# Value products and gates with features on partitions, and probabilities normalised ahead of their transposes, in a hybrid attention block

## What is computed

```python
h = rms_norm(x, norm_gain[l])
proj = jnp.einsum('btd,de->bte', h, w_in[l])
qa, ka, va, ga, qb, kb, vb, gb, qi, ki, wi = jnp.split(proj, offsets, axis=-1)
out_a = chunked_relpos_attention(heads(qa, H_A), heads(ka, H_A), heads(va, H_A), rel_bias[l])
out_b = dsa_sparse_attention(heads(qb, H_B), heads(kb, H_B), heads(vb, H_B), qi, ki, wi, slopes)
ya = out_a.reshape(B, T, D_A) * jax.nn.silu(ga)
yb = out_b.reshape(B, T, D_B) * jax.nn.silu(gb)
x = x + jnp.einsum('bte,ed->btd', concatenate([ya, yb]), w_out[l])
return rms_norm(x, final_gain)
```

## Time and profile before

| What | us |
|---|---|
| median of 3 runs | 533.62 (533.39 to 534.5) |
| span of the profiled execution, first to last instruction | 532.2 |
| median of the runs less that span | 1.4 |
| TensorE busy | 523.9 |
| VectorE busy | 351.6 |
| ScalarE busy | 262.7 |

### The profile page before, as it was taken

The page is one execution under the profiler, slowest core; times in us unless marked ns, Lnnn a source line. Parts: engine busy times, 40 slices in busy tenths (PEclk is TensorE's granted clock), DMA queues, the critical chain, the costliest instruction groups (busy, mean ns, idle before and its releaser), DMA issues.

```text
span 532.2 us, 8174 instructions
## 1 busy us (share of the span) xinstructions
PE 523.9 (98%) x2795; PEld 452.4 (85%) x2795; DVE 351.6 (66%) x516; ACT 262.7 (49%) x381; POOL 28.5 (5%) x46
## 2 busy tenths in 40 slices
PE   9999999999999999999999999999999999999994
PEld 6899998888888888888888888888888888888883
DVE  6897785765667656668665767657576666756454
ACT  6875545344543344445364636354545444634342
POOL 1005042250000000000000000000000000000000
PEclk9999999999999999999999999999999999999999
DMA  8966976659556566654655554555444574766614
GB/s 291 380 197 191 284 223 193 196 174 276 172 189 193 197 198 189 188 187 149 197 159 161 178 173 158 163 173 179 158 158 159 179 265 151 237 196 189 200 47 158
DMA packets 60375, 102.45 MB, mean 193 GB/s; under 512 B 3504, under 2 KB 45376, under 8 KB 60096
## 3 DMA queue, kind: packets, MB, share of 16 engines
q1 hardware_dynamic: 58656, 96.68, 56.6%
q0 software_dynamic: 1264, 5.00, 3.3%
q10 hardware_dynamic: 432, 0.47, 0.3%
HBM read 99.24 MB, written 2.11 MB: 190 GB/s over the span
## 4 chain that ended last, share of the span: by engine, by line
PE 98%; DVE 0%; ACT 0%; DVEq 0%; issue 0%
PE acc L427 27%; PE acc L392 16%; PE acc L394 16%; PE acc L393 16%; PE acc L425 13%; PE aux L613 1%; PE aux L503 1%; PE acc L430 1%; PE acc L464 1%; PE aux L617 1%; PE aux L592 1%; PE aux L674 1%; PE aux L602 1%; PE acc L440 1%; PE acc L449 0%; PE aux L590 0%
## 5 line engine op out<-in xcount | busy, mean ns | idle before, releaser
L988 DVE TENSOR_TENSOR w_lo<-w_raw,w_hi 128x1024 fp32r<-128x1024 f32 x172 | 213.4, 1243 | 151.3 <-ACT w_hi L717 150.5
L717 ACT ACTIVATE w_hi<-w_raw 128x1024 fp32r<-128x1024 f32 x172 | 181.9, 1059 | 224.0 <-PE acc L394 111.0
L427 PE MATMUL acc<-acts,w_hi 128*128 128x512 f32 (+1 forms) x640 | 215.5, 387 | 0.0
L425 PE MATMUL acc<-acts,w_lo 128*128 128x256 f32 (+1 forms) x600 | 165.4, 276 | 0.0
L392 PE MATMUL acc<-w_hi,acts 128*128 128x512 f32 x376 | 148.1, 394 | 0.0
L394 PE MATMUL acc<-w_hi,acts 128*128 128x512 f32 x376 | 146.6, 390 | 0.0
L393 PE MATMUL acc<-w_lo,acts 128*128 128x512 f32 x376 | 146.3, 389 | 0.0
L427 PEld LDWEIGHTS acc<-acts,w_hi 128*128 128x128 f32 x640 | 119.0, 188 | 20.2
L425 PEld LDWEIGHTS acc<-acts,w_lo 128*128 128x128 f32 x600 | 113.3, 189 | 0.7
L394 PEld LDWEIGHTS acc<-w_hi,acts 128*128 128x128 f32 x376 | 70.6, 188 | 15.1
L393 PEld LDWEIGHTS acc<-w_lo,acts 128*128 128x128 f32 x376 | 70.7, 188 | 14.2
(11 more groups left out here) (173 smaller groups left out, 364.6 us busy)
## 6 DMA issues: line engine op xcount, KB each, us to landing
w_raw<-w_blocks SPq DMA_DIRECT2D x140, 512.0 KB, 3.7
w_raw<-wo_blocks SPq DMA_DIRECT2D x32, 512.0 KB, 4.0
w_raw<-w_blocks SPq DMA_DIRECT2D x8, 256.0 KB, 5.8
v<-x POOLq DMA_DIRECT2D x1, 2048.0 KB, 10.2
qk<-xT SPq DMA_DIRECT2D x7, 256.0 KB, 6.5
o<-ext_dram POOLq DMA_DIRECT2D x1, 1024.0 KB, 7.2
fgain<-final_gain POOLq DMA_DIRECT2D x1, 1024.0 KB, 7.9
out<-o SPq DMA_DIRECT2D x2, 512.0 KB, 3.0
```

What stands on the lines that cost most here:

```text
L425: nc.tensor.matmul(acc[:, bank:bank + n], w_lo4[:, u % RING, q, c], a_hi[:, k, tokens], start=False, stop=False)
L427: last = nc.tensor.matmul(whole, w_hi4[:, u % RING, q, c], acts[:, k, :, tokens], start=(k == 0), stop=(k == KT - 1))
L717: nc.scalar.activation(flat(w_hi[:, s, :, :]), w_raw[:, s, :], ACT.Copy).then_inc(hi_done, 1)
L988: nc.vector.tensor_tensor(flat(w_lo[:, s, :, :]), w_raw[:, s, :], flat(w_hi[:, s, :, :]).bitcast(f32), ALU.subtract).then_inc(lo_done, 1)
```

## The change

- The gate blocks 14 to 17 are made in feature layout (`feature_unit`) and multiplied by `rk`; SP loads their weights in that layout.
- Probabilities are multiplied by one over their sums (`normalise`) ahead of their transposes. TensorE waits for this, not for the exponentials.
- v is kept as `v0_hi`, `v0_lo` (tokens 0 to 127, split) and `v1`. The value products have v as the stationary operand and give features on partitions: for each pair two full-precision products with `pT1` and six of 256 columns with `pT_hi` and `pT_lo`. ScalarE makes `pT_hi` and VectorE `pT_lo` (`pT_rest`).
- ScalarE copies the value products out, times 0.5 (`output`); `gated` works on features; `y_hi` and `y_lo` read `o` in SBUF. `y_transposes` is gone.
- In blocks 10 to 13 ScalarE takes exponentials before `features_low`. x is fetched into the storage of `qk` after the last score. TensorE's loops over blocks 10 to 17 are written out.

The diff, cut to its core:

```diff
...
-            def transpose_pair(pair, used2):
-                pe.wait_ge(exp_done, pair + 1)
-                pe.wait_ge(aux_read[2], used2)
+            def transpose_pair(pair):
+                pe.wait_ge(normed, pair + 1)
+                pe.wait_ge(aux_read[2], pair + AUX23_PAIRS)
...
+            def value_pair(pair):
                 pe.wait_ge(aux_read[1], pair + (AUX1_PAIRS + 1))
-                pe.wait_ge(aux_read[3], used3)
+                pe.wait_ge(aux_read[2], pair + (AUX23_PAIRS + 1))
+                pe.wait_ge(aux_read[3], pair + AUX23_PAIRS)
+                heads = [slice(2 * pair * HD + h * HD, 2 * pair * HD + (h + 1) * HD) for h in range(2)]
+                for h, c in enumerate(heads):
+                    nc.tensor.matmul(aux[3][:, h * T + P:h * T + T], v1_flat[:, c], pT1[:, h, :],
+                                     start=(h == 0), stop=False, skip_group_check=True)
+                for h, c in enumerate(heads):
+                    dst = aux[3][:, h * T:h * T + T]
+                    rows_hi, rows_lo = pT_hi[:, h * T:h * T + T], pT_lo[:, h * T:h * T + T]
+                    nc.tensor.matmul(dst, v0_hi_flat[:, c], rows_hi, start=False, stop=False, skip_group_check=True)
+                    nc.tensor.matmul(dst, v0_lo_flat[:, c], rows_hi, start=False, stop=False, skip_group_check=True)
+                    last = nc.tensor.matmul(dst, v0_hi_flat[:, c], rows_lo, start=False, stop=(h == 1),
+                                            skip_group_check=True)
                 last.then_inc(pv_done, 1)
...
             for u in range(UNITS):
                 pe.wait_ge(ylo_done, u + 1)
                 unit(G_OUT, u)
-                if u + 3 < UNITS:
-                    y_transposes(u + 3)
...
+            def pT_out(pair):
                 act.wait_ge(pt_done, pair + 1)
+                nc.scalar.activation(pT_hi, aux[2][:, :], ACT.Copy).then_inc(pt_hi_done, 1)
+                nc.scalar.activation(flat(pT1[:, :, :]), aux[1][:, 0:2 * P], ACT.Copy).then_inc(aux_read[1], 1)
...
             def gate_block(g, i, q_next):
                 split_hi(g, 6)
                 split_hi(g, 7)
                 exps(i + 4, False)
+                features_low(g, 0, 0)
                 split_hi(g, 8)
+                tanh_gate(i, 0)
                 split_hi(g, 9)
-                pT0_out(i + 4)
+                pT_out(i + 4)
                 if q_next is not None:
                     stage_q(q_next, q_next + 4, 8)
                 split_hi(g, 10)
+                split_hi(g, 11)
+                output(i + 4)
...
+            def y_hi(q):
+                act.wait_ge(y_done, q + 1)
+                act.wait_ge(mm_done, (G_OUT - 1) * UNITS + (6 if q < 4 else 8))
+                nc.scalar.activation(a_hi[:, UK * q:UK * q + UK, :],
+                                     o_flat[:, q * 2 * T:(q + 1) * 2 * T].rearrange("p (k t) -> p k t", k=UK),
+                                     ACT.Copy).then_inc(yhi_done, 1)
...
             gate_block(G_OUT - 1, 3, None)
...
+            for q in range(4):
                 y_hi(q)
+            features_low(G_OUT - 1, 1, 0)
+            for q in range(4, 7):
+                y_hi(q)
+            tanh_gate(3, 1)
+            split_hi(G_OUT, 4)
+            split_hi(G_OUT, 5)
+            y_hi(7)
...
+            def normalise(pair):
+
                 dve.wait_ge(exp_done, pair + 1)
                 nc.vector.reciprocal(flat(p_inv[:, :, :]), flat(p_sum[:, :, :])).then_inc(inv_done, 1)
                 dve.wait_ge(inv_done, pair + 1)
+                for t, p in enumerate((p1, p0)):
+                    for h in range(2):
+                        last = nc.vector.tensor_scalar(p[:, h, :], p[:, h, :], p_inv[:, t, h:h + 1], None, ALU.mult)
+                last.then_inc(normed, 1)
+
+            def pT_rest(pair):
+                dve.wait_ge(pt_hi_done, pair + 1)
+                nc.vector.tensor_tensor(pT_lo, aux[2][:, :], pT_hi.bitcast(f32),
+                                        ALU.subtract).then_inc(aux_read[2], 1)
...
+            def gate_block(g, i, next_pair):
                 split_lo(g, 6)
                 bias_a(i)
                 maxima(i + 4, False)
                 split_lo(g, 7)
+                normalise(i + 4)
+                gate_out(g, i, 0)
                 split_lo(g, 8)
-                pT1_out(i + 4)
+                gated(i, 0)
                 split_lo(g, 9)
+                pT_rest(i + 4)
                 split_lo(g, 10)
```

More of the change, by code:

```diff
@@ L603, in transpose_pair @@
                 for h in range(2):
-                    last = nc.tensor.transpose(aux[1][:, h * P:h * P + P], p0[:, h, :], ident[:, :])
+                    last = nc.tensor.transpose(aux[1][:, h * P:h * P + P], p1[:, h, P:T], ident[:, :])
                 last.then_inc(pt_done, 1)
-            def value_pair(pair, used2, used3):
-                pe.wait_ge(aux_read[2], used2 + 1)
+            def value_pair(pair):
                 pe.wait_ge(aux_read[1], pair + (AUX1_PAIRS + 1))
-                pe.wait_ge(aux_read[3], used3)
[L611 to L618, removed]
+                pe.wait_ge(aux_read[2], pair + (AUX23_PAIRS + 1))
[11 more added lines that the diff above has]
+                                            skip_group_check=True)
@@ L619, in value_pair @@
                 last.then_inc(pv_done, 1)
             pe.wait_ge(keys_out, 4)
-            with pe.Fori(0, 4) as i:
-                g = i + G_QKA
-                both_out(3)
+            for pair in range(HEADS):
+                g = pair + G_QKA
+                if pair == 0:
+                    both_out(3)
                 pe.wait_ge(feat_out, 2 * g - 9)
@@ L634, in _ @@
                 feature_unit(g, 5, 0)
-                transpose_pair(i, i + AUX23_B)
+                transpose_pair(pair)
                 feature_unit(g, 6, 0)
-                value_pair(i, i + AUX23_B, i + AUX23_B)
+                value_pair(pair)
                 feature_unit(g, 7, 0)
[L641 to L666, removed]
-                if q < 4:
-                    pe.wait_ge(aux_read[q], (AUX0_Y, AUX1_Y, AUX23_Y, AUX23_Y)[q])
-                else:
-                    pe.wait_ge(ylo_done, q - 3)
-                for kk in range(UK):
-                    for m in range(TM):
-                        c = (q % 2) * PAIR + kk * HD
-                        last = nc.tensor.transpose(aux[q % 4][:, kk * T + m * P:kk * T + m * P + P],
-                                                   o[:, q // 2, m, c:c + HD], ident[:, :])
-                last.then_inc(ytr_done, 1)
-            y_transposes(0)
-            unit(G_OUT - 1, 7)
-            y_transposes(1)
-            y_transposes(2)
-            both_out(token_count(G_OUT - 2))
+            pe.wait_ge(feat_out, 2 * G_OUT - 9)
             for u in range(UNITS):
@@ L891, in feature_attention @@
                 split_hi(g, 11)
+                output(i)
                 features_low(g, 1, 0)
```

189 lines of the change are left out of this document (89 added, 100 removed).

## The result

The changed kernel takes **541.33 us** (539.07 to 542.3, four executions) against 533.61 (533.39 to 534.5): ratio 1.0135, interval 1.012 to 1.015. In a second set it took 540.92 against 533.85, ratio 1.0137 (1.0122 to 1.0153). The forecast was 537.7 with a range up to 540.0. The direction was right and the time lies 3.6 us above the forecast, outside the range.

The account below looks back on a forecast made before the run. TensorE's instruction stream was taken to bound the kernel. Work −3.4, gate block waits +3.4, block 10 +0.9 and first output unit +3.2 summed to +4.1 us: 537.7, range 535.6 to 540.0.

Parts of the forecast that it names:

- What bounds the kernel: Whole kernel: TensorE never waits after its start, so time is its issue steps plus a short tail and any new waits.
- TensorE's own work: Layout, value products and transposes together: −3.4 us, giving 530.2 with no new wait.
- The layout: Gate blocks 14 to 17: feature layout costs 0.34 us more a block than token layout, +1.3 us for four.
- Value products: Each pair's group takes 1.15 us instead of 1.26, −0.11 each, −0.9 us for eight pairs.
- the transposes of y: Output blocks: eight groups of four transposes on gated results go, 0.48 us each, −3.8 us.
- Gate blocks: Value products wait 0.8 us for VectorE's remainder of the transposed probabilities in each of four blocks: +3.4 us, ends 1.6 and 5.0.
- Block 10: Transposes wait for the reciprocal and four scalings behind late exponentials: +0.9 us, ends 0.6 and 1.1.
- First output unit: After block 17, TensorE waits for y(0), queued behind slot 3's weight splits: +3.2 us, ends 2.6 and 3.7.
- no wait in blocks 11 to 13: Feature blocks: slack 0.8 us in 11 and 0.1 in 12 and 13, taken as nothing; up to 0.3 each for 12 and 13.
- rival 1: Gap before the output blocks: the clock falls to the 1.2 GHz level, costing 2.2 us more, 539.9; chance 0.08.
- the gate chain fits: Gate blocks: no wait there, TensorE waits only in block 10 and at the output, +0.7 us, 534.3; chance 0.07.
- all waits vanish: End of block 17 and gate chain: queues are ready in time, the matmul stream alone decides, 530.2; chance 0.05.

Follow-up runs that it names:

- three pieces moved: Changed kernel with y(0) to y(3) and the transposed probabilities' remainder put ahead of weight splits, and the bias table's reversal put later: 530.59 us, ratio 0.9939.
- the changed kernel again: The changed kernel timed once more with no edit, beside the kernel before: 540.92 us, ratio 1.0137.
- the remainder moved: Changed kernel with VectorE's remainder of the transposed probabilities put ahead of the weight split before it in four gate blocks: 536.49 us, ratio 1.0054.
- five products: Changed kernel with five unread products of 512 columns put on TensorE between block 17 and the first output unit: 540.83 us.
- y behind the split: Kernel before with ScalarE's high parts of y(0) and y(1) put behind both tanh and slot 3's weight split in the last gate block: 537.69 us, ratio 1.0076.

## Why the prediction was right and wrong

**What bounds the kernel** was right: TensorE's stream and the waits put into it account for the time, and with the waits taken out the time is the stream's.

**TensorE's own work**, forecast −3.4: measured −3.3 (530.59 against 533.91). The layout: three gate blocks without waits, 342.11 to 418.00, are 25.30 each against 25.05, 0.25 more where the two terms of the forecast came to 0.34 − 0.11 = 0.23. Value products: a feature block fell from 25.39 to 25.26, by 0.13; forecast −0.11. So the price of the layout from the rows held. The Trainium skill's rule ("TensorE: Matmul & The Clock Gate", Back-to-back issue gap) would have had 0.08 a block, for 32 more products at 2.5 ns each (an estimate; the forecast writes 0.09), and the runs do not agree with it: they show 0.34 and, by the blocks here, 0.25 + 0.13 = 0.38. Four gate blocks at +0.25 and four feature blocks at −0.13 leave 3.8 for the transposes of y, as forecast; the expectations above went by 3.5, and the medians are too coarse to decide between the two.

**The places of the waits** were all right, and so was the working that led to them. **Their sizes** were somewhat short. Gate blocks: 0.8 forecast, 1.04 measured, 4.2 in four (4.4 by the experiment) against 3.4. VectorE's chain was right to 0.07; what the sum left out is "and the signal", named and not priced, which is 0.10, and the slower start behind a wait, 0.08. Block 10: 0.9 forecast, 1.07 measured. The wait itself was right: from the first q_early product to the first transpose pass 250.36 − 239.96 = 10.40 us in the changed kernel and 249.63 − 240.12 = 9.51 with three pieces moved, 0.89 less. The rest, 0.15, again lies behind the wait: from that transpose to the next block's scores pass 16.78 and 16.63. First output unit: 3.2 forecast; from L426 to the second product, 442.77 − 438.95 = 3.82 against 434.06 − 433.81 and one step of 0.23, which is 3.3. The terms as measured give −3.3 + 4.2 + 1.1 + 3.3 = +5.3: 538.9 from 533.6, and the one execution without a fall took 539.07. So these sizes are 1.2 of the 3.6 us missed, and alone would have left the time inside the range.

**What was costed at nothing**: no wait in blocks 11 to 13, as taken. The v0 remainder, the earlier fetch of x and the loops written out add no row to the list of waits.

**The step that failed is rival 1, the clock**, at a chance of 0.08: the sum has no term for a fall of the clock in the stand before the output blocks. The fall came in three of four executions, and in all four of the second set. It was argued down by the earlier trace rows: in the tail the clock stayed at 1.00 through 4.4 us of idle TensorE, so 3.2 us seemed safe. That was one execution's value of something that varies. Here is the tail of the kernel with three pieces moved, whose last product starts at 520.92 and ends at 521.31:

```profile
521.30:523.50 2.20, 0.01 (x1) 0.00 (x0) 1.70 (x4) 1.17 (x4) 0.00 (x0) 1.00 0.54 214
523.60:528.50 4.90, 0.00 (x0) 0.00 (x0) 0.96 (x3) 0.58 (x1) 0.00 (x0) 0.50 0.57 214
```

The clock fell after 2.2 us of idle TensorE. In the ten profiles of this case the tail's fall comes 2.2 to 4.9 us after the end of the last product (4.6 in the kernel before, 3.6 in the changed kernel). The three profiled falls before the output blocks fit in: they come 3.1 us (the changed kernel again), 3.9 (the remainder moved) and 2.3 (five products) after TensorE had gone idle, and by then work had resumed 0.0, 0.7 and 0.4 us earlier. So a gap that ends before the fall is not safe from it, and with 1.9 us idle it came in three executions of five. Its price, 2.2 forecast, is 1.7. The Trainium skill (same page, Why this matters for your kernels) warns of such gaps, and the runs agree, down to 1.9 us: the warning deserved the larger chance.

With the clock as the likely case the forecast would have been 537.7 + 2.2 = 539.9, and 538.9 + 1.7 = 540.6 with the sizes as measured; the medians are 540.92 and 541.33. The range had room for the clock or for dearer waits, not for both. The last 0.3 to 0.7 us is within what executions differ by in their first 12 us, long before anything that the change touches. The kernel before, and the same kernel with y behind the split:

```profile
5.57 2.08 PE L449 MATMUL acc<-w_hi,acts 128*128 128x512 f32 x4
...
12.49 0.39 PE L392 MATMUL acc<-w_hi,acts 128*128 128x512 f32 x1
```

```profile
5.57 1.45 PE L449 MATMUL acc<-w_hi,acts 128*128 128x512 f32 x4
...
11.88 0.39 PE L392 MATMUL acc<-w_hi,acts 128*128 128x512 f32 x1
```

The same four products take 0.6 us longer in one of them, though the windows read a clock of 1.00 there in both. Over the ten profiles the first plain unit starts between 11.54 and 12.49.

**The other rivals.** That the gate chain fits was wrong by the four waits. That all waits vanish and 530.2 is left was wrong for this order and right as a number: with the order mended the time is 530.59.

What stays open: why the clock falls in some executions of a kernel and not in others with the same gap, and what made the two slowest executions of the first set (541.77 and 542.3) slower than one fall explains.

## What to carry to other kernels

When every engine's queue is fixed by hand, a change that saves work on the bounding engine should be costed in two sums, the work and the waits. Here −3.3 us of work was turned into +7.1 (540.92 against 533.85) by instructions that stood behind weight splits or a table set-up they did not need, and moving them gave the saving back. Look at what stands ahead of the first result that the next stage needs, above all where a split has to wait for the last product of the stage before.

Price a wait at its end too: the signal, the slower first products, and on TensorE the clock behind it. In this kernel a single idle stretch of 1.9 to 3.1 us cost 1.7 us more whenever the clock fell. Where such a stretch could not be removed, unread products in it cost little: 539.43 against 539.07 in the one execution of the changed kernel without a fall.

A single row can show that a thing happens, but not how far apart its values lie. Before a term is put at nothing by one row, read the same place in every execution at hand, and where there is only one, leave the rival a larger chance.

## What the runs showed of the hardware

- Judged by time and mean clock, the granted clock fell in 15 of 19 executions with a wait of 2.8 to 3.1 us (the changed kernel 7 of 8, the remainder moved 5 of 5, y moved in the kernel before 3 of 6), in 3 of 5 with 1.9, and in none of 4 where products filled the gap. Mean clock alone does not tell, since it takes in the tail: the profile with three pieces moved has 0.995 with no fall ahead of its tail. In the three profiles with a fall before the output blocks the clock stayed at 0.50 for about 3.4 us.
- The clock's fall in the tail came 2.2 to 4.9 us after the last product's end, in ten profiles.
- Behind the short waits it did not fall. The changed kernel's windows behind the wait of 0.81 in block 16:

```profile
408.00:409.00 1.00, 0.25 (x2) 0.28 (x3) 0.65 (x2) 1.00 (x1) 0.00 (x0) 1.00 0.47 163
409.00:410.00 1.00, 1.00 (x11) 1.00 (x11) 0.93 (x1) 0.04 (x1) 0.00 (x0) 1.00 0.59 160
```

- A wait of TensorE in a gate block cost 0.23 more than its row in the list says (1.04 against 0.81).
- The difference between an execution's time and its span was 2.00 to 2.13 us in every run. The forecast took 1.4 for it, from a median set beside the span of one execution; since terms were added to the same median this did not move the time.
